# Opening of a hybrid encoder layer: weight blocks, tables and idle products are issued in another order

## The reference, cut to what matters

```python
hn = _rmsnorm(x, norm_g)
proj = jnp.einsum('bsd,de->bse', hn, w_in)                 # 1024 -> 9216
q, k, v, z_a, hc, gb, gc, z_b, g = jnp.split(proj, ...)
# banded attention of three head groups (window, dilation) = (128,1), (512,4), (2048,16)
u = gc * hc
conv = conv_w[0] * up[:, :-2] + conv_w[1] * up[:, 1:-1] + conv_w[2] * up[:, 2:]
c = jnp.einsum('bsc,cd->bsd', jax.nn.silu(z_b) * (gb * conv), w_conv_out)
merged = g_a * a + g_c * c
return x + jnp.einsum('bsd,de->bse', merged, w_o)          # then _rmsnorm(h, final_g)
```

## Time and profile before

| | us |
|---|---|
| median of 3 runs (lowest, highest) | 1474.95 (1473.37, 1475.21) |
| the profiled execution's own time | 1475.51 |
| span of its slowest core (core 2) | 1474.0 |
| spans of the 8 cores | 1469.1 to 1474.0 |
| TensorE busy in the span | 1454.9 (99%) |
| VectorE, ScalarE, GpSimd busy | 887.3, 661.9, 177.6 |
| DMA queues, share of the 16 engines: POOL's (q0), SP's (q1) | 22.8%, 21.9% |

### The profile page before, as it was taken

The page is one execution under the profiler, slowest core; times in us unless marked ns, Lnnn a source line. Parts: engine busy times, 40 slices in busy tenths (PEclk is TensorE's granted clock), DMA queues, the critical chain, the costliest instruction groups (busy, mean ns, idle before and its releaser), DMA issues.

```text
span 1474.0 us, 30550 instructions; the slowest of 8 cores (1469.1 to 1474.0 us)
## 1 busy us (share of the span) xinstructions
PE 1454.9 (99%) x13201; PEld 848.2 (58%) x13245; DVE 887.3 (60%) x1194; ACT 661.9 (45%) x1011; POOL 177.6 (12%) x320
## 2 busy tenths in 40 slices
PE   7999999999999999999999999999999999999998
PEld 5756765665655544444455767877776444444443
DVE  4677473473573896554466458394765967433357
ACT  4667455555455422443232556565655311222234
POOL 3452000000010010232011101000100100000000
PEclk9999999999999999999999999999999999999999
DMA  9673234143154141999295524425341522222157
GB/s 227 171 163 84 59 76 70 20 92 54 20 101 78 28 74 22 170 161 205 41 300 152 118 61 66 93 37 73 69 66 31 86 52 42 31 34 44 22 195 261
DMA packets 109994, 138.16 MB, mean 94 GB/s; under 512 B 69362, under 2 KB 69394, under 8 KB 109860
## 3 DMA queue, kind: packets, MB, share of 16 engines
q0 software_dynamic: 27728, 54.65, 22.8%
q1 hardware_dynamic: 82132, 81.56, 21.9%
HBM read 145.97 MB, written 23.66 MB: 115 GB/s over the span
## 4 chain that ended last, share of the span: by engine, by line
PE 96%; DMA 3%; DVE 1%; SPq 0%; issue 0%; ACT 0%; DVEq 0%; ACTq 0%; POOLq 0%
PE ps L456 87%; PE ps L468 8%; DMA Y<-xw 2%; DMA wbf<-wblk 1%; PE ps L483 1%; SPq L487 0%; DVE Y L420 0%; DVE hnT L444 0%; DVE Y L411 0%; ACT Y L443 0%; DVE Y L444 0%; DVEq L1383 0%; ACT Y L407 0%; ACT stat L1191 0%; PE ps L690 0%
## 5 line engine op out<-in xcount | busy, mean ns | idle before, releaser
L456 PE MATMUL ps<-hnT,wbf 128*128 128x512 bf16 (+4 forms) x5648 | 1025.0, 338 | 4.7 <-DMA wbf<-wblk 3.5
L456 PEld LDWEIGHTS ps<-hnT,wbf 128*128 128x128 bf16 x5648 | 523.2, 98 | 444.1 <-DMA wbf<-wblk 3.8
L407 ACT ACTIVATE Y<-ps 128x1024 bf16<-128x1024 f32 (+1 forms) x292 | 240.8, 872 | 192.4 <-PE ps L456 143.9
L443 ACT ACTIVATE Y<-ps 128x512 bf16<-128x512 f32 (+1 forms) x304 | 181.1, 597 | 275.1 <-PE ps L456 253.7
L411 DVE TENSOR_TENSOR Y<-ps,Y 128x512 f32<-128x512 f32 (+1 forms) x196 | 125.7, 673 | 203.8 <-PE ps L468 170.5
L420 DVE SCALAR_TENSOR_TENSOR Y<-Y,ps 128x512 f32<-128x512 f32 x192 | 130.8, 683 | 167.9 <-PE ps L456 149.0
L487 POOL DMA_DIRECT2D wbf<-wblk x160 | 86.9, 544 | 962.3 <-PE ps L456 945.9
L407 ACT ACTIVATE Y<-ps,cf 128x512 f32<-128x512 f32 x128 | 87.6, 686 | 218.2 <-PE ps L456 205.3
L411 DVE TENSOR_TENSOR Y<-Y,et 128x1024 bf16<-128x1024 bf16 x192 | 129.8, 685 | 15.6 <-ACT Y L407 11.3
L407 ACT ACTIVATE Y<-Y 128x1024 bf16<-128x1024 f32 (+3 forms) x83 | 85.9, 1035 | 115.6 <-DVE Y L420 86.0
L468 PEld LDWEIGHTS ps<-Y 64*128 64x128 bf16 x4640 | 114.5, 94 | 31.4 <-issue 26.3
(11 more groups left out here) (48 smaller groups left out, 424.0 us busy)
## 6 DMA issues: line engine op xcount, KB each, us to landing
wbf<-wblk POOLq DMA_DIRECT2D x160, 256.0 KB, 4.9
Y<-xw SPq DMA_DIRECT2D x56, 512.0 KB, 7.9
Y<-xw SPq DMA_DIRECT2D x48, 256.0 KB, 7.0
y<-Y POOLq DMA_DIRECT2D x16, 512.0 KB, 4.3
y<-Y SPq DMA_DIRECT2D x15, 512.0 KB, 5.1
Y<-wblk POOLq DMA_DIRECT2D x16, 256.0 KB, 7.5
et<-etab SPq DMA_DIRECT2D x8, 384.0 KB, 3.7
cv<-Y SPq DMA_DIRECT2D x4, 768.0 KB, 5.1
```

The costliest lines, as they stand in the source:

```text
L407: R.add("act", [lambda e: e.activation(out=out.a, in_=in_.a, func=func, scale=scale, **kw)], c_act(in_.n) + (0.2 if accum is not None else ...
L443: return e.activation(out=out.a, in_=in_.a, func=AF.Copy)
L456: fns = [(lambda e, m=m: e.matmul(m[0].a, lhsT=m[1].a, rhs=m[2].a, start=m[3], stop=m[4])) for m in mms]
```

## The change

It does five things: the identity moves from the SP queue to the head of the POOL queue; the weight blocks V and K are issued behind the identity's landing; the two tables are issued behind tile 2, between the weight blocks gc and zb; the idle products after g's go from 13 times 2 to 6 times 2; and the planner's model of the two DMA queues gets other numbers, with the two tables at a cost of 0.1.

```diff
-        dma_free = {"sp": 5.3, "pool": 5.3}
+        dma_free = {"sp": 2.2, "pool": 5.0}
...
                 begin = max(t0 + cost, dma_free[n])
-                if n == "pool" and 5 < t0 < 28:
-                    begin = max(t0 + cost + 3.7, dma_free[n])
-                us = o.dma[1] * (1.0 if begin > 42 else 1.15 if begin < 7 or begin > 30 else 1.9 if n == "pool" else 1.75)
+                us = o.dma[1] * (1.0 if begin > 42 or begin < 3 else 1.15 if begin > 26 else 1.75)
...
-        wload(0, (2, 1))
         R.add("dve", [lambda e: e.memset(cf.cols(CF_MH, 1).a, -0.5)], 0.1, [], [cf.cols(CF_MH, 1)])
         R.add("dve", [lambda e: e.memset(cf.cols(CF_EPS, 1).a, EPS)], 0.1, [], [cf.cols(CF_EPS, 1)])
         dma("sp", g_in.a, bass.AP(gvec, 0, [[D, 1], [1, D]]), [], [g_in], 0.1)
-        dma("sp", ident.a, bass.AP(cbf_d, 384, [[512, 128], [1, 128]]), [], [ident], 0.1)
-        f_in, pat_in = cf.cols(CF_CW, 32), cbf.cols(0, 384)
-        dma("pool", f_in.a, cfp_d.ap(), [], [f_in], 0.2)
-        dma("pool", pat_in.a, bass.AP(cbf_d, 0, [[512, 128], [1, 384]]), [], [pat_in], 0.3)
+        wload(0, (2, 1), behind=dma("pool", ident.a, bass.AP(cbf_d, 384, [[512, 128], [1, 128]]), [], [ident], 0.1))
         warm(4)
...
-        for _ in range(13):
+        for _ in range(6):
             warm(2)
         xload = [ln_own(0, None)]
         wload(0, (0,), behind=xload[0])
         for p in (1, 2, 3):
             xload.append(ln_own(p, None))
             wload(1, ((0, 1, 3)[p - 1],), behind=xload[p])
+            if p == 2:
+                for o, src in ((cf.cols(CF_CW, 32), cfp_d.ap()),
+                               (cbf.cols(0, 384), bass.AP(cbf_d, 0, [[512, 128], [1, 384]]))):
+                    dma("pool", o.a, src, [], [o], 0.1).deps.add(xload[2].i)
```

## The result

| | before | after |
|---|---|---|
| median of the runs compared, us | 1474.95 | 1482.32 and 1485.54 |
| ratio, 95% interval | | 1.0064 (1.0033 to 1.0094) |
| profiled execution's own time | 1475.51 | 1482.32 |
| span of the slowest core | 1474.0 (core 2) | 1480.7 (core 4) |
| mark on that core, rest behind it | 38.76, 1435.2 | 43.14, 1437.6 |

The change makes the kernel slower by about half a per cent: the interval lies above 1, and both times lie above the prediction's whole range, 1470.6 to 1479.2. The same kernel measured again, with four executions that count instead of two, gave 1.0053 (1.0038 to 1.0069).

A forecast was written before the change was run, and what follows sets the result against it. The opening bounds the kernel, through the slowest core's mark. Edge table landing at 26.5, plus 1.1, 10.5 of work and 1.1 of slow clock, puts the mark at 39.2 against 38.76: 1475.9 us, range 1470.6 to 1479.2.

The forecast's parts named there:

- The bound and the mark: Opening decides; mark is the start of chunk 1's run of 96 products, 38.76 us on core 2; rest equal within 1.4.
- Identity and first tile: Opening DMAs: tile 0, issued 0.4 us earlier, could land 2 to 3 us earlier; no gain booked in itself.
- V: Weight block on POOL's queue: issued at 4.3 behind the identity, takes 7.5 us, lands at 11.8 against 9.6.
- rival 1: Opening: tables hold nobody up, block gb decides, landing at 31.6; mark 34.3, time 1471.1; chance 25%.
- The other blocks and the tables: POOL queue: blocks 3.13 us apart, edge table lands at 26.5; VectorE waits with tile 3's copies behind it.
- the rival that went by it: Rival 1 (25%): by the skill page's 2.2 us the tables land near 15 and no one waits for them.
- The sum: Opening: edge table 26.5, then 1.1 to tile 3's products, 10.5 work, 1.1 slow clock; mark 39.2, time 1475.9.
- Fewer idle products: TensorE's opening: 14 fewer idle products, 3.1 us fall out; costed at nothing, covered by the wait for tile 0.
- rival 2: VectorE at the CF_HB operation: same wait, longer; edge table at 29.4, mark 42.7, time 1479.4; chance 22%.

## Why the prediction was wrong

**The bound and the mark.** Right as a way of reading: the opening decides first. That the rest "is the same length everywhere within 1.4 us" held for the kernel before and was carried over without reason. After the change it is 1432.8 to 1437.6, and the slowest core of after has 2.4 of its 6.7 us over the slowest of before there. The planner orders the whole kernel anew when costs in its opening change, and the prediction gave the planner's numbers no cost at all; but since the rest reaches 1437.2 in the order of before too, how much of the 2.4 the order brings is not shown.

**Identity and first tile.** Tile 0 landed earlier than forecast, at 5.2 to 6.9. Its sum of squares at "7 or 8" held on two cores and not on the six where ScalarE was held up by g. That it would bring nothing was right. The identity's landing, "I take 4.3, near the short row", is the step at which the sum began to go wrong: it landed at 5.4 to 7.2, and V was issued at 6.07 on core 4 and up to 7.79 elsewhere, past the upper bound of 6.0. The bound came from a transfer on idle engines, and here it shared them with tile 0.

**V.** "I take 7.5" from issue to products; it was 10.7 (16.78 minus 6.07), more than the 9.7 given as the end. With the identity's 1.8 that makes V 5.0 us late against the forecast 11.8. This is the mis-sized term. That late blocks cost by themselves, without any table, was not in the sum: the program with V and K behind the identity and early tables lost 0.29% and, measured again, 0.22%. It loses through gb, the last block, which lands some 3 us later, and less through K and a long time at half clock. The prediction had the path through gb only in rival 1, with gb at 31.6; it landed at 34.6 to 36.1, and its path alone gives marks of 37.4 to 38.8.

**The other blocks and the tables.** From V to the edge table the prediction has 12.5 + 2.2 = 14.7 us; it was 30.96 minus 16.78 = 14.2. The queue's even spacing, the place in VectorE's order and the planner's blindness all held, the last one shown by telling it a later landing. (In the kernel before the edge table was the fourth DMA of its queue, not the third; the 16 KB of `cfp` stood ahead of it too. Nothing hangs on it.)

The Trainium skill's page "DMA: Bandwidth & Descriptors", section "Anatomy of one DMA — SWDGE (gpsimd) path", gives, as an estimate from its fixed time and rate for one DMA, 2.1 us for the identity and 2.2 us for the edge table; the trace has 3.9 and 16.1 on core 4. So the measurement decides against it here, where other transfers were under way, and the rival that went by it is refuted.

**The sum.** "Time = landing of the edge table + 1449.4" gives 1480.4 with the measured 30.96. Its parts were 1.0 from the landing to tile 3's products (1.1 forecast), 11.2 from there to the mark (10.5 + 1.1) and 1437.6 + 1.6 behind it (1435.2 + 1.5). The 11.2 is 9.84 us of work at the full clock, as on the cores without half clock, and 1.3 for the clock; so core 3's 10.5 was somewhat too long for it and the 1.1 somewhat too short. Of 6.4 us that the profiled run is above the forecast (1482.3 against 1475.9), 4.5 are the landing; behind the mark 2.5 are lost, and 0.5 are won between the two.

**Fewer idle products.** "I cost it at nothing; the cover is the wait for tile 0." With V and K issued at once that holds at the mark (mean 36.1 against 36.3). Behind a late V the cover is gone: on core 2 of the kernel after the idle products end at 9.1 and TensorE then waits 1.8 us for tile 0 and 6.2 for V. Half clock in the opening, summed over the eight cores from where their records of it begin, is 75 us in the kernel after, 55 with the numbers of before, 44 with 13 pairs as well, 10 in the kernel before. Putting the pairs back did not help where it was tried with the new numbers (1.0037 against 1.0031 with early tables), so the price of this term stays open.

**The rivals.** It was rival 2, "the same wait, longer", which had 22% and 1479.4; its condition (identity near 5, V 9.7) was met and passed. Its 1479.4 was still 2.9 short: 1.6 in the landing (29.4 against 30.96), whose ends came from rows in which SP's queue was less far ahead, and 2.5 behind the mark, less 1.1 between the two.

What stays open is how the 0.2 to 0.3% between the whole change and its DMAs alone divide. Going back with the numbers alone gives 1.0039, with idle products too 1.0031; the intervals overlap, and the one run with all DMAs moved, the new numbers and 13 pairs is among the two that decide nothing. What the traces do show is where the opening differs: with the old numbers no core of sixteen has half clock behind the wait for tile 3, with the new ones nine of sixteen have, and the marks reach 44.3 and 45.7 instead of 42.3. Why the clock falls there and not behind a wait of 3.43 us with all DMAs moved (core 2, 32.43) is not known.

## What to carry to other kernels

A transfer that is taken off the start of a shared queue does not arrive later by its own time but by that of the backlog it now stands behind (landing at 13.9 to 15.3 us before, at 29.2 to 31.4 after); bound it by the worst row, and ask who in the fixed order of an in-order engine reads it. Follow the queue to its last transfer as well: a late start at its head came out at its end, and TensorE's mark hung on that last block on all eight cores of two runs here. Do not hold back bulk loads for the landing of a small one: put it ahead of them in the queue, which cost at most 0.17% here (1.0008, interval from 0.9999) against 0.2 to 0.3% for the wait (0.1 to 0.2% with the small load on the faster queue). Waits that end in one place do not add; compare the paths and take the later. Where a planner with estimated costs orders the program, an edit to the first microseconds is an edit to all of it: measure such an edit once with the old order kept, and compare the two orders before reading a cause from the sum of single edits.

## What was not expected of the hardware

The same 32 KB landed 1.6 to 2.6 us after issue from SP, in the eight kernels that issue it there, and 3.7 to 6.1 us from POOL in the twelve other profiled executions. Two of them differ in that alone (tables at once, V and K behind the identity): 1.8 to 2.4 us from SP, 3.8 to 6.1 from POOL.

Small shifts in the first two microseconds came back larger. With the identity at the head of POOL's queue V was issued 0.7 us later and tile 0 0.4 us earlier than before; V landed 3.6 us later and tile 0 3.5 earlier, on the mean of the cores, and gb, six blocks on, was still 1.8 us late. From 7 to 16 us POOL's queue moved 0.57 MB on core 4 before, when its blocks were issued at 1.56, and 0.36 when they were issued at 6.07; SP's moved 1.70 and 1.86.

TensorE's clock fell to 1.2 GHz in or behind waits of mostly 1.8 to 6.2 us in the opening and again at single waits of 2.1 to 3.7 us between 130 and 142 us, though not at all of them. It stayed full behind 3.43 us here, core 2 with all DMAs moved:

```profile
32.43 1.51 PE L456 MATMUL ps<-hnT,wbf 128*128 128x128 bf16 x24 [3.43 <-DVE hnT L444]
```

And from none to six of the eight cores of an execution start slowly: their products of 512 columns follow each other every 0.43 us until 13 to 14 us, and every 0.22 us from about 5 us on the others. The kernel after had six such cores, four and none in its three profiled executions.
